# One block instead of four in a one-core decoder layer, the first norm on three-operand VectorE steps, and the residual scaled on ScalarE

## The reference

```
rq,rk,rv,rg,fq,fk,fv,ff,ga,gb = split(x @ w_in)
logf = log_sigmoid(ff + b_f)
fox  = softmax attention (8 heads of 64) with cumulative logf bias; samples attend to 4096 paged cache rows
ret  = chunkwise retention (4 heads, 128 x 256 state), group norm, times silu(rg)
mix  = (sigmoid(ga) * (ret @ w_pa) + sigmoid(gb) * (fox @ w_pb)) @ w_o
h    = layer_norm(ALPHA * x + mix, ln1_w, ln1_b)
u, gt = h @ w_up, h @ w_gate                      # 1024 -> 2816
f    = (gelu(causal_conv3(u)) * gt) @ w_down
y    = layer_norm(ALPHA * h + f, ln2_w, ln2_b)
```

## Time and profile before

| | |
|---|---|
| three runs | 2094.16, 2096.11, 2099.72 us; median 2096.11 |
| the profiled execution's own time | 2099.52 us |
| its span, first to last instruction | 2097.8 us |
| mean granted TensorE clock | 0.983 |
| PE matmul busy / weight load busy | 1969.2 us (94%) / 1841.5 us (88%) |
| DVE / ACT / POOL busy | 1144.9 (55%) / 652.7 (31%) / 224.8 us (11%) |
| DMA | 276.50 MB, mean 132 GB/s |

### The profile page before, as it was taken

How to read it: one execution, slowest core, us unless ns; L and a number is a source line. 1 busy time by engine, 2 the same in 40 slices (tenths; PEclk the granted TensorE clock), 3 DMA queues, 4 the chain that set the end, 5 groups by cost and what they waited for, 6 DMA issues and landing times.

```text
span 2097.8 us, 38511 instructions
## 1 busy us (share of the span) xinstructions
PE 1969.2 (94%) x14335; PEld 1841.5 (88%) x14335; DVE 1144.9 (55%) x1747; ACT 652.7 (31%) x1211; POOL 224.8 (11%) x254
## 2 busy tenths in 40 slices
PE   7899998799999999989899998899999999999996
PEld 5787897798888888878799996899999999999996
DVE  3555454877867876885433846633322333233348
ACT  4454444134133223313411303632211322123234
POOL 0000000020020020020000100500000000100005
PEclk8999999999999999999999999999999999999999
DMA  3211201787988888886832411111111111111154
GB/s 121 72 32 31 61 21 47 242 308 252 314 273 289 270 273 293 275 309 236 283 109 92 122 50 31 31 41 50 50 40 50 40 49 44 48 50 40 38 161 134
DMA packets 151698, 276.50 MB, mean 132 GB/s; under 512 B 19057, under 2 KB 57966, under 8 KB 151558
## 3 DMA queue, kind: packets, MB, share of 16 engines
q1 hardware_dynamic: 115954, 175.22, 25.1%
q0 software_dynamic: 23264, 82.83, 13.0%
q10 hardware_dynamic: 12368, 16.88, 2.2%
HBM read 247.24 MB, written 27.72 MB: 131 GB/s over the span
## 4 chain that ended last, share of the span: by engine, by line
PE 45%; DVE 3%; ACT 1%; DMA 1%; issue 0%; SPq 0%; ACTq 0%; DVEq 0%
PE bank L121 42%; PE bank L1706 2%; DVE w_lo L2061 1%; DMA gated_raw<-gated_t_scratch 1%; DVE y L2037 0%; DVE ln_stats L2046 0%; DVE z L1957 0%; DVE x_lo L1974 0%; PE bank L1646 0%; ACT z L1770 0%; PE bank L1667 0%; ACT gate L1761 0%; ACT moving_hi L1718 0%; ACT x_hi L1772 0%; PE banks L1667 0%
## 5 line engine op out<-in xcount | busy, mean ns | idle before, releaser
L121 PE MATMUL bank<-x_hi,w_hi 128*128 128x344 f32 (+1 forms) x1896 | 617.7, 326 | 35.7 <-DVE rot_sin L1299 14.4
L121 PE MATMUL bank<-x_lo,w_hi 128*128 128x344 f32 (+1 forms) x1896 | 608.5, 321 | 0.0
L121 PE MATMUL bank<-x_hi,w_lo 128*128 128x344 f32 (+1 forms) x1896 | 608.4, 321 | 0.0
L121 PEld LDWEIGHTS bank<-x_hi,w_hi 128*128 128x128 f32 (+1 forms) x1896 | 356.5, 188 | 52.1 <-issue 32.6
L121 PEld LDWEIGHTS bank<-x_hi,w_lo 128*128 128x128 f32 (+1 forms) x1896 | 356.5, 188 | 1.8 <-issue 0.3
L121 PEld LDWEIGHTS bank<-x_lo,w_hi 128*128 128x128 f32 (+1 forms) x1896 | 356.5, 188 | 1.7 <-issue 0.2
L97 ACT ACTIVATE w_hi<-w_raw 128x1024 fp32r<-128x1024 f32 (+3 forms) x139 | 141.8, 1020 | 407.4 <-PE bank L121 366.2
L121 PE MATMUL bank<-moving_lo,w_hi 128*128 128x344 f32 x744 | 237.5, 319 | 0.0
L121 PE MATMUL bank<-moving_hi,w_hi 128*128 128x344 f32 x744 | 225.3, 325 | 4.8 <-DVE moving_hi L1868 2.5
L104 DVE TENSOR_TENSOR w_lo<-w_raw,w_hi 128x1024 fp32r<-128x1024 f32 (+3 forms) x139 | 164.4, 1182 | 96.3 <-ACT w_hi L97 95.0
L121 PE MATMUL bank<-moving_hi,w_lo 128*128 128x344 f32 x648 | 208.1, 321 | 0.0
(11 more groups left out here) (297 smaller groups left out, 2855.7 us busy)
## 6 DMA issues: line engine op xcount, KB each, us to landing
cache_keys<-in_cache_k_dram SPq DMA_DIRECT2D x256, 256.0 KB, 4.8
cache_vals<-in_cache_v_dram SPq DMA_DIRECT2D x256, 256.0 KB, 5.2
w_raw<-in_w_in_dram POOLq DMA_DIRECT2D x52, 512.0 KB, 6.2
w_raw<-in_w_up_dram POOLq DMA_DIRECT2D x22, 512.0 KB, 4.5
w_raw<-in_w_gate_dram POOLq DMA_DIRECT2D x22, 512.0 KB, 4.5
tail_raw<-in_w_down_dram SPq DMA_DIRECT2D x22, 448.0 KB, 3.7
gate<-gate_t_scratch SPq DMA_DIRECT2D x15, 516.0 KB, 3.5
w_raw<-in_w_down_dram POOLq DMA_DIRECT2D x10, 448.0 KB, 4.3
```

The source lines that it names most:

```text
L121: mm = pe.matmul(g.bank[n][0:m, 0:TC], w[slot][:, k, 0:m], x[:, k, chunk(n)], start=(k == 0 and i == 0), stop=(k == kt - 1 and i == 2))
```

## The change

It does three things.

1. The four functions no longer open blocks: each returns its five engine programs, and one block runs them one behind the other on each engine. Where the blocks' ends had ordered the work, waits on semaphores stand: PE's first product of `fox` waits chunk by chunk for the ACT copies of `dec_bias`; in `retain` ACT waits for the stores of `fox` before its first weight split, DVE behind its first weight split and ahead of its memsets, SP ahead of the first key load; SP takes over from ACT the wait for the gated and gate stores, now ahead of the read-back, and no longer waits for its own store of the sample rows there, but ahead of the load that needs them. POOL's memset of `over` moves behind the w_pa loads. The DVE program at the start of `fox` is put in another order.
2. First norm: `scale` becomes z times weight times 1/root in one DVE step, ACT writes the high part in one step (plus bias), and `h_low` becomes (z + bias) - high in one DVE step. The mean is subtracted from all three chunks before DVE splits the gate weight. So 24 ACT steps go.
3. POOL no longer scales the residual. In the first section ACT makes `acc` tile by tile, ALPHA * z + ALPHA * bias, one step of 1032 columns in each of 8 tiles, ahead of that tile's gelu. `conv_cols` gets a 21st column that holds ALPHA * bias. The up product of tile 1 waits only for the up banks of tile 0 (`freed=ju + 2`), and its weight is split earlier in tile 0.

The diff, without the change of indentation, cut to its core:

```
@@ product @@
-def product(g, pe, jb, xh, xl, kt=KD, m=P, before=None, ready=None, after=None):
+def product(g, pe, jb, xh, xl, kt=KD, m=P, before=None, ready=None, after=None, freed=None):
-        pe.wait_ge(g.bank_free[n], j + 1)
+        pe.wait_ge(g.bank_free[n], j + 1 if freed is None else freed)
@@ prepare @@
-                act.activation(g.conv_cols[:], bank[3][:, 0:FT * 20]...
+            act.activation(g.conv_cols[:, :, 0:20], bank[3][:, 0:FT * 20]...
-                            sums[n][:, :]...[:, b], ACT.Copy)
+                        sums[n][:, :]...[:, b], ACT.Copy).then_inc(g.bias_out, 1)
@@ fox: sync @@
-                sp.wait_ge(fo_stored, 2 * NIT * 16)
                 for u in range(2):
                     sp.wait_ge(kv_stored[u], NIT * 32)
+            sp.wait_ge(lf_turned, 1)
@@ fox: tensor @@
-                            product(g, pe, job(it * 6 + 1, 1, j), g.xh, g.xl)
+                        product(g, pe, job(it * 6 + 1, 1, j), g.xh, g.xl,
+                                before=None if pair or w else lambda n: pe.wait_ge(g.bias_out, 4 * n + 4))
-                        pe.wait_ge(parts_ready, 1)
@@ fox: vector @@
-                dve.memset(ones[:], 0.0).then_inc(sum_chain, 1)
-                dve.wait_ge(sum_chain, 1)
-                ch = Chain(dve, sum_chain, 1)
-                for r in range(2):
-                    ch.link(dve.tensor_copy(k2[own(1 - r), r, :], ones[own(1 - r), :]))
+            ch = Chain(dve, sum_chain)
                 ch.link(dve.memset(ones[:], 1.0))
                 ch.link(dve.tensor_tensor_scan(cum[:], ones[0:FH, :], g.lf[:, 0:SEQ], 0.0, ALU.mult, ALU.add))
                 ch.link(dve.tensor_scalar(cum[:], cum[:], -1.0, None, ALU.mult))
+            split_lo(g, dve, job(1, 1, 1))
+            ch.link(dve.memset(ones[:], 0.0))
+            dve.wait_ge(g.bias_mm, 4)
+            for r in range(2):
+                ch.link(dve.tensor_copy(k2[own(1 - r), r, :], ones[own(1 - r), :]))
+            ch.link(dve.memset(ones[:], 1.0))
...
+                        if pair or w:
                             split_lo(g, dve, job(it * 6 + 1, 1, 3 * u + w + 1))
@@ retain: sync @@
                 load_q(1, 1)
+            sp.wait_ge(g.fo_stored, FH // 2 * 16)
...
-                sp.wait_ge(fos_stored, 16 * (FH // 2))
+            sp.wait_ge(turned, NS)
+            sp.wait_ge(g_stored, RH * 32)
+            for b in range(2):
+                sp.wait_ge(gate_stored[b], stored_until(b, RH - 1, 12))
+            sp.wait_ge(st_stored, RH * 16)
+            sp.wait_ge(fin_stored, RH * 16)
@@ retain: scalar @@
+            act.wait_ge(g.fo_stored, FH // 2 * 16)
+            for u in range(2):
+                act.wait_ge(g.kv_stored[u], FH // 4 * 32)
                 split_hi(g, act, job(J0, 1, 1))
...
-                act.wait_ge(g_stored, RH * 32)
-                for b in range(2):
-                    act.wait_ge(gate_stored[b], stored_until(b, RH - 1, 12))
-                act.wait_ge(st_stored, RH * 16)
-                act.wait_ge(fin_stored, RH * 16)
@@ retain: vector @@
                 dve.wait_ge(const_land, 48)
+            dve.wait_ge(g.fo_stored, FH // 2 * 16)
+            dve.wait_ge(g.lf_out, 1)
@@ finish: sync @@
                 for i in range(KD - 1):
                     load_gate(i)
+            sp.wait_ge(g.fos_stored, 16 * (FH // 2))
@@ finish: gpsimd @@
-                pool.memset(over[:], 1.0 / D).then_inc(over_set, 1)
...
+            wait_apart(pool, s_hi, KD, g.mm_chunk)
+            pool.memset(over[:], 1.0 / D).then_inc(over_set, 1)
...
-                        up_and_gate(1, f0, ju)
-                        for k in range(NCH):
-                            pool.wait_ge(h_full, (k + 1) * KD)
-                            pool.wait_ge(h_lo, (k + 1) * KD)
-                            for t in range(KD):
-                                ins = pool.tensor_scalar(acc[:, t, chunk(k)], z[:, t, chunk(k)], ALPHA, None, ALU.mult)
-                            ins.then_inc(h_scaled, 1)
-                    with pool.Fori(2 if s == 0 else 0, n) as i:
+                with pool.Fori(1 if s == 0 else 0, n) as i:
@@ finish: tensor @@
+            up_and_gate_of(1, 0, ju, freed=ju + 2)
@@ finish: scalar @@
-                        act.activation(z[:, k, chunk(n)], z[:, k, chunk(n)], ACT.Identity, scale=ln_cols[:, 0, k:k + 1], bias=ln_cols[:, 1, k:k + 1]).then_inc(h_full, 1)
-                        act.wait_ge(h_full, n * KD + k + 1)
-                        act.activation(g.xh[:, k, chunk(n)], z[:, k, chunk(n)], ACT.Copy).then_inc(h_hi, 1)
+                    act.activation(g.xh[:, k, chunk(n)], z[:, k, chunk(n)], ACT.Identity, bias=ln_cols[:, 1, k:k + 1]).then_inc(h_hi, 1)
...
+            act.activation(g.conv_cols[:, 0:KD, 20:21]..., ln_cols[:, 1, :], ACT.Copy, scale=ALPHA).then_inc(h_scaled, 1)
+            act.wait_ge(h_scaled, 1)
+            act.wait_ge(h_lo, NCH * KD)
...
+                    if first:
+                        act.wait_ge(g.mm_chunk, NCH * (RING + ju) + 2 * NCH - 1)
+                        split_hi(g, act, job(i * 2 + ju, ju % 2, 2))
...
+                    if s == 0:
+                        act.activation(acc[:, ds(i, 1), :]..., z[:, ds(i, 1), :]...,
+                                       ACT.Identity, scale=ALPHA, bias=fc[:, 20:21]).then_inc(h_scaled, 1)
+                        act.wait_ge(h_scaled, i + 2)
@@ finish: vector @@
                 centre(0)
-                split_lo(g, dve, job(JF, JF % 2, 1))
                 centre(1)
                 centre(2)
+            split_lo(g, dve, job(JF, JF % 2, 1))
...
-                    dve.tensor_tensor(z[:, k, chunk(n)], z[:, k, chunk(n)], rstd[:, chunk(n)], ALU.mult).then_inc(normed, 1)
+                dve.scalar_tensor_tensor(z[:, k, chunk(n)], z[:, k, chunk(n)], ln_cols[:, 0, k:k + 1], rstd[:, chunk(n)], ALU.mult, ALU.mult).then_inc(normed, 1)
...
-                    dve.tensor_tensor(g.xl[:, k, chunk(n)], z[:, k, chunk(n)], g.xh[:, k, chunk(n)].bitcast(F32), ALU.subtract).then_inc(h_lo, 1)
+                dve.scalar_tensor_tensor(g.xl[:, k, chunk(n)], z[:, k, chunk(n)], ln_cols[:, 1, k:k + 1], g.xh[:, k, chunk(n)].bitcast(F32), ALU.add, ALU.subtract).then_inc(h_lo, 1)
...
+                    else:
+                        split_lo(g, dve, job(i * 2 + ju, ju % 2, 2))
```

2871 lines of the change are left out of this document (1445 added, 1426 removed).

## The result

The changed kernel takes 0.9944 of the time before, 95% interval 0.9933 to 0.9956: 11.7 us less. The medians are 2085.4 us of 18 runs against 2097.4 of 18, which lie 12.0 apart. The forecast was 2076.9 us, in a range of 2070.0 to 2088.0, and faster. The direction and the range held; the expected gain, 19.2, was 7 too large. The two profiled executions lie further apart than the medians: 2099.52 and 2081.49 us, 18.0. So the first question is which part of those 18 us belongs to the change at all.

A forecast was written before the change was run, and what follows sets the result against it. PE, busy 94% of the span, was taken as the bound, so only its waits could shrink. Terms 2.9 + 5.5 + 3.0 + 7.8 = 19.2 us, taken from the median 2096.11, gave 2076.9, range 2070.0 to 2088.0.

The forecast's parts named there:

- The start: End of prepare: without the block's end fox's second product starts 3.4 us earlier, less 0.5 for early loads; gain 2.9.
- The fear that the loads hold up x: Rival at the start: early weight loads delay the x tiles, part 1 is worth 0.4, result 2079.4; chance 0.14.
- that rule alone: At the start: POOL's early loads take turns with x tiles on the same 16 DMA engines; gain only 0.4.
- The end of fox: Fox to retain: the first key step moves from 376.56 to about 370.7; gain 5.5, ends 2.3 and 8.2.
- 3.4 us, the median landing of pages in this stretch, bring it to 370.6: End of fox: first page group, issued at 367.2, lands 3.4 us later, so the key step comes 5.9 us earlier.
- All of it moves: Head loop: PE's 14.4 us of rotation waits follow DVE's chain, which shifts whole where DVE sets the pace.
- The end of retain: Retain to finish: read-back starts 1.9 us earlier, and an early w_pa load saves 1.3; gain 3.0, ends 0 and 4.3.
- it is bound by bytes, and one of two w_pa loads leaves before it: End of retain: the read-back is limited by bytes, so the earlier 0.5 MB load saves 1.3 us.
- My lower end: End of retain, gain 0: the stores land late, and PE's waits between slices cost clock.
- The norm: First norm: tile 1 starts 6.0 us earlier and 1.8 us of clock loss go; gain 7.8, ends 3.6 and 10.2.
- The semaphores take the place of the blocks: Rival: PE's head start at the three block ends is given back at the next transfer; gain 8.8, 2087.3; chance 0.17.
- as worked out: Whole kernel: the terms hold as computed, gain 12 to 26 us; chance 0.56.

The follow-up runs named there:

- joined kernel: The changed kernel, or a variant of it, without the block boundary at the stage in question; the changed kernel itself took 0.9944, repeated 0.9952.
- the first boundary of before: Block boundary between prepare and fox with DVE's old order: two profiles of the kernel before, one of that kernel with the new norm alone (0.9949).
- the first profile of before: First profiled execution of the unchanged kernel, 2099.52 us; a repeat of that kernel with its own profile measured 2096.43 us, ratio 0.9997.
- the first changed profile: First profiled execution of the changed kernel, 2081.49 us; a repeat with its own profile measured 2084.14 us, ratio 0.9952.
- The gates held: Changed kernel with SyncE holding the first two gate tiles until all eight gated tiles are split: 2082.2 us, ratio 0.9931.
- the kernel with the sigmoid ahead: Changed kernel with gate tiles held, second sample's query loaded behind first keys, and ScalarE's first held-gate sigmoid ahead of the gated tiles: 2084.21 us, 0.9939.

## Why the prediction was right, and where it was too high

**The start** (forecast 2.9). From `logf` to the second product every joined kernel gains 2.7 us. The column as a whole says 3.1, with chance in it: nine joined kernels whose loads leave early gain 6.0 us on the mean at 75 us, the three profiles with the first boundary of before 2.9 (0, 4.0, 4.8). The working held in its parts: DVE's chain starts at `logf`'s end, costs one memset more, the weight wait is gone. The fear that the loads hold up x, a rival at 0.14, did not come true to any size that shows. The Trainium skill (DMA: Bandwidth & Descriptors, "Issuing engines are not separate DMA queues") has the loads of all engines interleave; that agrees with PE's new wait of 1.04 us for an x tile at 23.08. But by that rule alone the prediction had the start worth 0.4. The last x tile was turned at 24.70, between the first profile of before, 25.70, and the second:

```profile
23.11 0.65 PE L250 MATMUL bank<-ident,x_stage 128*128 128x128 f32 x4 [0.39 <-DMA x_stage<-in_x_prompt_dram]
```

A comparison with one of these two profiles alone could have been read either way.

**The end of fox** (forecast 5.5, measured 2.7: 2.8 on the mean of the seven joined kernels less 0.1 on that of the four profiles with this boundary). The times say 2.3, not clear of noise. The step that failed is "3.4 us, the median landing of pages in this stretch, bring it to 370.6". That median is taken over 22 pages issued up to 400 us, and the later ones land in about 3. The first eight took 3.8 to 6.8 us in the very profile that I read, median 4.9, and a group is there only when its second page is, which is issued half a microsecond behind the first. In the kernel before, that made 6.0 us from the first issue (369.52) to the landing of the second page (375.49); in the changed kernel it was 5.1. With 6.0 the same working gives 373.2 for the first key step, 3.4 earlier than 376.56 and not 5.9; the first changed profile gained 4.1 at that step, and the mean of the seven joined kernels 3.5. The stretch is full in the changed kernel too:

```profile
356.00:360.00 4.00, 4.00 (x27) 4.00 (x26) 1.30 (x3) 0.77 (x1) 0.88 (x1) 1.00 0.97 322
```

I had taken 1 MB of weights off it, and it was filled by the queries, the next weight (POOL at 358) and the pages themselves. A lead of 3.5 us at the first key step is 2.8 at 600 us. "All of it moves" was right for DVE's step; PE's waits on the rotation, from 352 to 640 us, stayed at 11.0 and 12.3 us (12.0 in both profiles of before), as forecast, and what PE lost in waits is its own for the block, 2.69.

**The end of retain** (forecast 3.0, measured a loss of 1.4: -1.5 on the mean of seven joined kernels, -0.1 on that of four with the boundary). This is the step that failed by sign: "it is bound by bytes, and one of two w_pa loads leaves before it". From the first issue to the last landing the read-back took 16.8 us in the kernel before and 16.8 in the changed one, so this load bought nothing. And it began only 1.0 us earlier (1021.19 and 11.1 make 1032.3, against 1033.26) where I had 1.9: SP's stores ended at 1020.27, and the wait for the gated stores, which I took for nothing, held SP until 1021.13. The last of the eight tiles is not bound by the bytes of all eight. It is issued 10 us behind the fourth (1032.81 against 1022.50), when ACT has split the fourth; by then SP's next instructions, two gate loads, follow within 0.4 us and share the engines with it. In the kernel before, too, they do, but PE then runs its first product beside the read-back; in the joined kernel that product is done at 1029.4, and PE waits in pieces, 6.3 us in all, and runs from 1040 to 1044 us at a granted clock of 0.57. Of the 6.3, 2.5 are a wait for ACT's first sigmoid, whose table load of 1.28 us stands between two tiles. In the time of before (the execution was 11.1 ahead at 1025 us) the last gated split ends at 1051.4: 1.0 earlier than 1052.43, where I had forecast about 1049, and the clock takes that back and more. My lower end named this ("PE's waits between slices cost clock") and gave it a term of 0; the gain I worked with had no price for it. The gates held turn the loss into 2.8.

**The norm** (forecast 7.8, measured 8.2). The steps held: 0.50 per three-operand step, pairs 0.98 apart, DVE the bound, ACT's residual hidden, full clock behind; the first reciprocal came 0.7 later than forecast (1296.2 for 1295.5 in the time of before). The prediction leaves one thing unsaid: in the kernel before, GpSimd's multiplies ran beside DVE's second chunk, where five subtractions took 0.78 us that take 0.51 elsewhere, and its chain of waits runs through them. How much of the 8.2 is owed to GpSimd's silence is not shown.

The sum by the table is 3.1 + 2.7 - 1.4 + 8.2 = 12.6 us (12.2 with the 2.7 for the start), against 11.7 (9.2 to 14.1) and 10.1 (7.1 to 12.8) measured. Nothing large is left over. "The semaphores take the place of the blocks", my rival at 8.8, describes the last join; at the first two PE kept its head start. The case "as worked out" (12 to 26) missed the measured value by little. The time fell into the range by help of its width: of the four terms two were right, and two, 8.5 us together, gave 1.3. One more mistake was of another kind: I subtracted the terms from one profiled execution and moved the result to the median by 3.4, as if the difference were spread evenly. It lay in the start, between 15 and 35 us, the very stretch that I was costing. That did no harm to this term (it was built from the block's end on), but the comparison of the two first profiles made the start look like 6.8. A slip of small size: the third term's parts, 1.9 and 1.3, make 3.2, and not 3.0.

**What stays open.** Whether early loads lower the chance of the slow start. How the norm's 8.2 divide between the order of its steps, the bank condition and GpSimd's multiplies. Why the end of fox gives 1.3 to 4.0 in kernels that are equal there. The read-back with a different order of slots or a fifth landing slot was not tried: the tiles' place in memory overlaps buffers that the last gated store still reads.

## What to carry to other kernels

When a barrier goes, ask of each engine what it does with the time, and then which transfer is issued last ahead of the next product and what is issued right behind it: here two loads that nobody needed for 8 us (issued at 1033.17, first used at 1041.66) cost, by the table, more than the barrier had. Time won ahead of a wait is kept only if what ends the wait moves too. When a landing time goes into a sum, take it for the transfers that stand there and not over a longer window, and count to the last transfer of the group. And price a term of 3 us against two profiles of the kernel before, not one: unchanged stages differed by up to 4.8 us between executions.

## What the runs showed of the hardware

- The same instructions ran from 24 to 32 us once at a granted clock of 1.00 and once at 0.76 and 0.50, with a PE stall of 3.07 us ahead of the second. With both, the start differed by 5.6 us between two executions of one program.
- A three-operand VectorE step with a pointer scalar on 128 x 344 fp32 runs every 0.50 us (8 in 3.99), where the two-operand one runs every 0.44 (8 in 3.51): the third operand costs 14%.
- While GpSimd multiplied 128 x 344 fp32 tiles, five of VectorE's two-operand subtractions of that size took 0.78 us; with GpSimd idle they took 0.50 to 0.52. It repeats in all three profiles with the old norm.
- Of two executions of the changed kernel, the second lost 1.9 us more at the same place, where PE waits for the gated tiles in several pieces. In the kernel with the sigmoid ahead, splitting the wait in pieces didn't protect the clock at this place: 0.50 behind six waits, the longest 1.2 us.
